# Heads loop of a gated delta rule: recurrence steps, set-up and output norms in another order on all engines

## The reference

```python
L = jnp.where(strict, jnp.einsum('bhncd,bhnsd->bhncs', kb, k) * decay, 0.0)
T = lax.linalg.triangular_solve(eye + L, eye, left_side=True, lower=True, unit_diagonal=True)
u = T @ vb
w = T @ (kb * jnp.exp(g)[..., None])
attn = jnp.einsum('bhncd,bhnsd->bhncs', q, k) * decay
def step(state, inp):
    v_new = u_n - w_n @ state
    o = q_n @ state + a_n @ v_new
    state = state * gl_n + k_n.T @ v_new
o = rmsnorm(o, norm_w) * zg
```

## Time and profile before

| | |
|---|---|
| median of 3 runs | 1715.41 us |
| the profiled execution | 1713.06 us, its span 1711.3 us |
| TensorE busy | 1639.7 us, 96% |
| VectorE, ScalarE, GpSimd busy | 1124.1, 918.6, 489.2 us |
| granted TensorE clock | 0.996 of full in the mean |
| first product of the loop | 220.87 us |
| first output product behind it | 417.41 us |

### The profile page before, as it was taken

One profiled execution on the slowest core, in us unless ns is written; L12 is line 12 of the kernel. 1 busy time (PEld: TensorE's weight loads), 2 busy tenths in 40 slices (PEclk: granted clock), 3 DMA queues, 4 the chain that ended last, 5 costly groups with the idle time before them and its releaser, 6 DMA issues.

```text
span 1711.3 us, 33895 instructions
## 1 busy us (share of the span) xinstructions
PE 1639.7 (96%) x11715; PEld 1523.3 (89%) x11715; DVE 1124.1 (66%) x2320; ACT 918.6 (54%) x1712; POOL 489.2 (29%) x406
## 2 busy tenths in 40 slices
PE   7999999999999989999999999999999999999998
PEld 6899888898988879988999999999999988888886
DVE  4776355554655656367548999978889655555554
ACT  2665523333455555455445444479889744554554
POOL 3000054452700000400006777776666300000000
PEclk9999999999999999999999999999999999999999
DMA  9665411114735324514844555554444456555553
GB/s 295 206 193 174 137 36 50 40 36 144 236 114 148 100 87 149 178 62 137 197 98 137 171 168 167 168 165 134 139 135 140 155 194 195 191 192 194 195 189 131
DMA packets 211817, 255.66 MB, mean 149 GB/s; under 512 B 15912, under 2 KB 193804, under 8 KB 211724
## 3 DMA queue, kind: packets, MB, share of 16 engines
q1 hardware_dynamic: 211723, 254.39, 48.4%
HBM read 253.29 MB, written 1.05 MB: 149 GB/s over the span
## 4 chain that ended last, share of the span: by engine, by line
PE 63%; issue 18%; POOL 10%; DVE 4%; ACT 3%; DMA 1%; SPq 1%; POOLq 0%; DVEq 0%; ACTq 0%
PE ps L2670 20%; PE ps L2108 13%; PE ps L2652 9%; POOL w_lo L716 9%; PE ps L2640 3%; PE ps L2285 3%; PE ps L2284 2%; PE ps L2369 2%; PE ps L2272 2%; PE ps L2128 1%; PE ps L2202 1%; PE ps L2445 1%; DMA arena<-in_ada_w 1%; POOL arena L706 0%; SPq L452 0%
## 5 line engine op out<-in xcount | busy, mean ns | idle before, releaser
L716 POOL TENSOR_TENSOR w_lo<-raw,w_hi 128x1024 fp32r<-128x1024 f32 x128 | 307.8, 2408 | 333.0 <-ACT w_hi L1188 332.8
L2108 PE MATMUL ps<-x_hi,w_hi 128*128 128x256 f32 x1088 | 312.7, 287 | 8.3 <-DVE w_lo L1310 3.0
L2108 PE MATMUL ps<-x_lo,w_hi 128*128 128x256 f32 x1088 | 307.7, 283 | 0.0
L2108 PE MATMUL ps<-x_hi,w_lo 128*128 128x256 f32 x1088 | 307.7, 283 | 0.0
L2067 DVE TENSOR_TENSOR w_lo<-raw,w_hi 128x1024 fp32r<-128x1024 f32 x124 | 152.0, 1226 | 143.3 <-ACT w_hi L1288 143.3
L1288 ACT ACTIVATE w_hi<-raw 128x1024 fp32r<-128x1024 f32 x124 | 131.6, 1061 | 168.0 <-PE ps L2670 168.0
L2108 PEld LDWEIGHTS ps<-x_hi,w_hi 128*128 128x128 f32 x1088 | 208.4, 192 | 14.0 <-issue 4.7
L2108 PEld LDWEIGHTS ps<-x_lo,w_hi 128*128 128x128 f32 x1088 | 208.6, 192 | 0.3 <-issue 0.2
L2108 PEld LDWEIGHTS ps<-x_hi,w_lo 128*128 128x128 f32 x1088 | 208.4, 192 | 0.0
L1188 ACT ACTIVATE w_hi<-raw 128x1024 fp32r<-128x1024 f32 x128 | 134.9, 1054 | 118.1 <-DVE raw L1879 118.1
L2615 PE MATMUL ps<-x_hi,w_hi 128*128 128x256 f32 x576 | 166.2, 288 | 9.9 <-ACT arena L1210 8.9
(11 more groups left out here) (416 smaller groups left out, 3822.4 us busy)
## 6 DMA issues: line engine op xcount, KB each, us to landing
raw<-in_u_experts SPq DMA_DIRECT2D x512, 128.0 KB, 2.6
raw<-in_v_experts SPq DMA_DIRECT2D x128, 512.0 KB, 4.3
arena<-in_ada_w SPq DMA_DIRECT2D x22, 1024.0 KB, 5.3
raw<-in_a_w_in SPq DMA_DIRECT2D x12, 1024.0 KB, 5.4
arena<-in_a_w_in SPq DMA_DIRECT2D x12, 1024.0 KB, 5.4
raw<-in_b_w_in SPq DMA_DIRECT2D x8, 1024.0 KB, 5.7
arena<-in_b_w_in SPq DMA_DIRECT2D x8, 1024.0 KB, 5.5
raw<-in_w_in SPq DMA_DIRECT2D x8, 1024.0 KB, 5.5
```

What stands on the lines that cost most here:

```text
L716: pool.tensor_tensor(UTL[e], UT[e % 2], UTH[e].bitcast(F32), ALU.subtract).then_inc(utl_ready, 1)
L2108: ins = mm(o[:, b * S:b * S + S], w[:, slot, kk, b * P:b * P + P], xx[:, (kk + turn) % KC, :], start=(kk == 0 and n == 0), stop=(kk == k - ...
```

## The change

The same operations are done, in another order. TensorE starts a round with the level-0 products and does the recurrence at levels 0 to 3: step 0 behind the products of level 0, steps 1 and 2 behind the updates of levels 0 and 1, step 3 behind the products of level 2, steps 4 and 5 behind the updates of levels 2 and 3. The keys come at level 1, the rows at level 2, the values at level 3, the modulator between the products and updates of level 4, and x0 between those of level 5. The eight clock-keeping matmuls of round 0 are gone. VectorE follows: keys at level 1, decays and betas at level 2, lower triangles and starts at level 3, the modulator and the first head's norm at level 4; the second head's norm comes in the next round behind the masks of level 0. ScalarE has its two sequences interleaved. The outputs (OS), the norms (RNo) and the exponentials of the decays (EG) have buffers of their own, and the value transposes go to banks 6 and 7. The zeroing of the mask buffer stands ahead of the key norms. The split of the first eight heads goes from round 7's VectorE and ScalarE to GpSimd in round 7 and ScalarE at the end of round 6.

```diff
-        temp(512)
+        EG = [temp(128), temp(128)]
+        OS = [temp(256)]
...
-        SQo = RNo = VN
+        SQo = VN
...
+        OS.append(temp(256))
+        RNo = [temp(256)]
...
+        RNo.append(temp(256))
...
-                    pool.tensor_tensor(QD[r.side][g], QD[r.side][g], r.q[:, 128:256], ALU.mult).then_inc(h_qd, 1)
+                    pool.tensor_tensor(QD[r.side][g], EG[g], r.q[:, 128:256], ALU.mult).then_inc(h_qd, 1)
 
             scores(Round(0))
             for i in range(GQ):
+                if i + 1 == GQ:
+                    for half in range(2):
+                        ks = slice(half * KC // 2, (half + 1) * KC // 2)
+                        pool.wait_ge(xhi_ready, 2 + half + 1)
+                        pool.tensor_tensor(XLO[:, ks, :], ZB[:, ks, :], XHI[:, ks, :].bitcast(F32), ALU.subtract).then_inc(x_split, 1)
...
-            def setup_rows(r):
+            def setup_keys(r):
                 act.wait_ge(g_k0, r.count(1, 1))
                 act.activation(K0, ps[7][:, 0:128], ACT.Copy).then_inc(g_k0s, 1)
                 if r.at:
                     act.wait_ge(h_at, r.count(2))
                 act.activation(KQs, two(ps[7][:, 256:512]), ACT.Copy).then_inc(g_kqs, 1)
+
+            def setup_rows(r):
+                if r.at:
+                    act.wait_ge(h_qd, r.count(2))
                 for g in range(2):
                     act.wait_ge(h_row, r.nth(g))
-                    act.activation(QD[r.side][g], ROWS[g][:, 128:256], ACT.Exp).then_inc(h_eg, 1)
+                    act.activation(EG[g], ROWS[g][:, 128:256], ACT.Exp).then_inc(h_eg, 1)
+
+            def setup_decays(r):
...
-                        act.activation(two(BV[r.side][g])[:, cc, :], A2[g][:, cc * 128:cc * 128 + 128], ACT.Copy,
+                        act.activation(two(BV[r.side][g])[:, cc, :], ROWS[g][:, 256 + cc * 128:384 + cc * 128], ACT.Copy,
...
-            def finish_states(r):
+            def finish_first(r):
...
+            def finish_second(r):
...
             def finish_out(r):
+                if r.at:
+                    act.wait_ge(h_out, r.count(2, 2))
                 for g in range(2):
                     act.wait_ge(h_o, r.nth(g))
-                    act.activation(OS[r.side][g], A2[g], ACT.Copy).then_inc(h_os, 1)
+                    act.activation(OS[g], A2[g], ACT.Copy).then_inc(h_os, 1)
                     act.activation(SQo[g], A2[g], ACT.Square).then_inc(h_sq, 1)
+
+            def finish_norms(r):
...
             def inner(i, f, n):
                 if f:
-                    finish_states(f)
+                    finish_first(f)
+                if n:
+                    setup_keys(n)
+                    setup_rows(n)
+                if f:
+                    finish_second(f)
+                if n:
+                    setup_decays(n)
                 if f:
                     finish_out(f)
                 if n:
-                    setup_rows(n)
                     setup_v(n)
-                    if f:
-                        act.wait_ge(h_out, f.count(2, 4))
+                if f:
+                    finish_norms(f)
+                if n:
                     setup_x0(n)
+                if i.at == GQ - 2:
+                    act.wait_ge(h_out, 2 + GQ)
+                    split_x(1, ZB[:, 0:8, :], 24)
 
             act.wait_ge(g_norm, 4 + 2 * GQ)
+            setup_keys(Round(0))
             setup_rows(Round(0))
+            setup_decays(Round(0))
             setup_v(Round(0))
             setup_x0(Round(0))
             act.wait_ge(raw_free, 8 + N_ADA)
             rounds(inner)
-            act.wait_ge(h_out, 2 + GQ)
-            split_x(1, ZB[:, 0:8, :], 24)
             hi(T_AOUT, 0, 1)
-            finish_states(Round(GQ - 1))
+            finish_first(Round(GQ - 1))
+            finish_second(Round(GQ - 1))
             finish_out(Round(GQ - 1))
+            finish_norms(Round(GQ - 1))
...
+            v.wait_ge(lo_ready, tile_no(T_AOUT, 0, 0))
+            v.memset(zeroed, 0.0)
...
-            def normed(r):
-                for g in range(2):
-                    v.wait_ge(h_orn, r.nth(g))
-                    v.wait_ge(h_os, r.nth(g))
-                    os_ = OS[r.side][g]
-                    v.scalar_tensor_tensor(os_, os_, COLS[:, CAN:CAN + 1], RNo[g], ALU.mult, ALU.mult).then_inc(h_og, 1)
-                for g in range(2):
-                    v.wait_ge(h_og, r.nth(g, 1, 1, 2))
-                    zb = ZB[:, r.heads[g], :]
-                    v.tensor_tensor(zb, OS[r.side][g], zb, ALU.mult).then_inc(h_out, 1)
+            def normed(r, g):
+                v.wait_ge(h_orn, r.nth(g))
+                v.wait_ge(h_os, r.nth(g))
+                v.scalar_tensor_tensor(OS[g], OS[g], COLS[:, CAN:CAN + 1], RNo[g], ALU.mult, ALU.mult).then_inc(h_og, 1)
+                v.wait_ge(h_og, r.nth(g, 1, 1, 2))
+                zb = ZB[:, r.heads[g], :]
+                v.tensor_tensor(zb, OS[g], zb, ALU.mult).then_inc(h_out, 1)
...
             def inner(i, f, n):
                 mask_level(i, 0)
+                if f and f.at:
+                    normed(Round(f.at - 1), 1)
                 close_level(i, 0)
                 mask_level(i, 1)
+                if n:
+                    keys(n)
+                close_level(i, 1)
                 if f:
                     remainder(f)
-                close_level(i, 1)
                 mask_level(i, 2)
+                if n:
+                    decays(n)
                 close_level(i, 2)
+                if n:
+                    betas(n)
                 mask_level(i, 3)
                 if n:
-                    keys(n)
+                    lowers(n)
                 close_level(i, 3)
-                if f:
-                    normed(f)
-                mask_level(i, 4)
-                if n:
-                    decays(n)
-                    betas(n)
-                close_level(i, 4)
-                if n:
-                    lowers(n)
-                else:
-                    split_x(1, ZB[:, 0:8, :])
-                mask_level(i, 5)
                 if n:
                     starts(n)
+                mask_level(i, 4)
+                modulator(i)
+                if f:
+                    normed(f, 0)
+                close_level(i, 4)
+                mask_level(i, 5)
                 close_level(i, 5)
-                modulator(i)
 
             v.sem_inc(h_out, 2)
-            v.memset(zeroed, 0.0)
...
             lo(T_AOUT, 0, 1)
+            normed(Round(GQ - 2), 1)
             remainder(Round(GQ - 1))
-            normed(Round(GQ - 1))
+            for g in range(2):
+                normed(Round(GQ - 1), g)
...
-                    pe.wait_ge(h_eg, r.count(2))
-                    pe.wait_ge(h_xm, r.count(4))
+                    pe.wait_ge(h_bv, r.count(4))
...
-            def setup_values(r, f):
+            def setup_values(r):
+                for g in range(2):
+                    pe.wait_ge(h_eg, r.nth(g))
+                    pe.wait_ge(h_xm, r.nth(g, 1, 0, 2))
+                    for cc in range(2):
+                        ins = pe.transpose(ROWS[g][:, 256 + cc * 128:384 + cc * 128], r.v[g][:, cc * 128:cc * 128 + 128], ident)
+                    ins.then_inc(h_vT, 1)
+
+            def setup_x0(r, f):
                 for g in range(2):
                     if f:
                         pe.wait_ge(h_orn, f.nth(g))
-                    for cc in range(2):
-                        ins = pe.transpose(A2[g][:, cc * 128:cc * 128 + 128], r.v[g][:, cc * 128:cc * 128 + 128], ident)
-                    ins.then_inc(h_vT, 1)
-
-            def setup_x0(r):
-                for g in range(2):
-                    pe.wait_ge(h_bv, r.nth(g, 2))
...
-                    pe.wait_ge(h_xm, n.nth(0, 1, 0, 2))
+                    pe.wait_ge(h_bv, n.nth(0, 2))
...
             def inner(i, f, n):
+                level_p(i, 0)
                 if f:
                     finish(f, 0, i)
-                level_p(i, 0)
+                level_d(i, 0)
                 if f:
                     finish(f, 1)
-                level_d(i, 0)
+                level_p(i, 1)
+                if n:
+                    setup_keys(n)
+                level_d(i, 1)
                 if f:
                     finish(f, 2)
-                level_p(i, 1)
-                level_d(i, 1)
+                if n:
+                    setup_rows(n)
+                level_p(i, 2)
                 if f:
                     finish(f, 3)
-                level_p(i, 2)
+                level_d(i, 2)
                 if f:
                     finish(f, 4)
-                level_d(i, 2)
+                level_p(i, 3)
+                if n:
+                    setup_values(n)
+                level_d(i, 3)
                 if f:
                     finish(f, 5)
-                if f is None:
-                    keep_clock(ps[7][:, 0:P], 8)
-                level_p(i, 3)
+                level_p(i, 4)
```

(17 more changed lines are left out.)

6 lines of the change are left out of this document (2 added, 4 removed).

## The result

The changed kernel takes 1694.76 us in the median of four runs (1694.15 to 1695.60), the kernel before 1715.28 us beside it (1714.07 to 1715.84). The ratio is 0.9881, with a 95% interval of 0.9869 to 0.9893: 20.5 us faster, and 1.8 us above the forecast. The profiled execution took 1694.15 us with a span of 1692.1 us, so the two profiles differ by 19.2 us of span.

A forecast was written before the change was run, and what follows sets the result against it. TensorE was taken to bound nearly everywhere. Start 1.76, round 0 3.53, rounds 1 to 6 13.0, round 7 3.62, output products 0.35 and tile 3 0.37 sum to 22.6 us: from 1715.41 to 1693, range 1688 to 1703.

The forecast's parts named there:

- The steady round: Rounds 1 to 6: 22.45 us each in place of 24.62, 2.17 us less, 13.0 us over six rounds.
- the two named ones: Stalls in a steady round: 0.27 us at level 4's updates, 0.34 us between updates 4 and products 5.
- By a hair: Level 4: first head's norm ends at 19.15 us, closing 4 is due at 19.17, so it costs nothing.
- Round 0: First round, without recurrence or clock-keeping products: 20.44 us against 23.97, 3.53 us less.
- I take full clock: Round 0: the clock is assumed not to fall; if it does, 1.2 us come back.
- The start: Ahead of the loop: moving the 1.76 us mask-buffer fill into VectorE idle time brings the first product 1.76 us earlier.
- Round 7: Last round to the first output product: 21.2 us against 24.82, 3.62 us less.
- does meet GpSimd and may take 1.6 us in place of 0.85: Second head's late norm, behind mask 0: ends at 3.0 us, closing 0 at 3.4, before products 1 at 3.57; hidden.
- Nothing, by half a us: GpSimd's split in round 7 costs nothing: sums end at 15.4 to 15.5 us, modulator due at 16.0.
- Rival 2: Clock falls in round 0 or at the end, or round 7 waits for GpSimd's split: 1695 us; chance 0.16.
- GpSimd's end: Steady round: GpSimd works until 13.3 us or so, 3 us before the starts on VectorE.
- Output products and tile 3: After the loop: 0.35 us from output products at full clock, 0.37 us from tile 3's shorter wait for weights.

The follow-up runs named there:

- experiment 7: Changed kernel with TensorE's x0 transposes put back behind the updates of level 5: 1699.62 us, ratio to before 0.9919.
- experiment 8: Changed kernel with recurrence step 0 put back in front of the level-0 products: 1699.32 us, ratio to before 0.9923.
- experiment 6: Changed kernel with both heads' norms behind the modulator at level 4, none behind mask 0: 1692.38 us, ratio to before 0.9878.
- experiment 4: Changed kernel with the zero fill of the mask buffer put back behind the key norms: 1696.37 us, ratio to before 0.9891.
- experiment 1: Changed kernel with GpSimd's split of round 7 behind its last sums in place of in front: 1691.52 us, ratio to before 0.9861.
- experiment 2: Changed kernel with GpSimd's split in the same place, cut into eight operations in place of two: 1689.57 us, ratio to before 0.9859.
- experiment 5: Changed kernel with GpSimd's split of round 7 as one operation in place of two: 1694.74 us, one run (before 1713.23).
- experiment 9: Changed kernel with GpSimd's split behind its sums and x0 between updates 4 and products 5: 1691.04 us, ratio to before 0.9860.
- experiment 10: Changed kernel with round 0's eight clock-keeping matmuls back in front of the products of level 3: 1694.78 us, ratio to before 0.9886.
- experiment 12: Changed kernel with GpSimd's split behind its last sums, measured again beside the changed kernel (1694.57 us): 1693.12 us, ratio to before 0.9870.
- the last set: The third set of runs, experiments 9 to 12, which includes the changed kernel itself (1694.57 us); the kernel before took 1714.59 us.
- experiment 3: Changed kernel with the zero fill of the mask buffer directly in front of the key norms: 1694.69 us, ratio to before 0.9887.

## Why the prediction was right, and where not

- **The steady round** was right by its steps: 22.375 us for 22.45. The stalls left are the two named ones (level 4's was 0.21 us for 0.27). That the others went for the named reasons is shown by putting two of them back: x0 (experiment 7) 0.72 us, step 0 (experiment 8) 0.62 us a round. "By a hair" for the first head's norm is shown by experiment 6.
- **Round 0**: 20.41 for 20.44. "I take full clock" held, with the clock-keeping products or without.
- **The start**: 1.59 us for 1.76, and 1.97 in experiment 4. The waits shrank as said, but the clock fell even so, in front of x0 instead of behind it. It fell in five of the thirteen profiles behind the change (both of the changed kernel, experiments 1, 2 and 4) and held in eight. It cost 0.46 us: from the fill's start to the first product it is 31.25 us in the changed kernel, and 30.79 in experiments 5 to 10 and 12, whose clock held.
- **Round 7 is the step that failed**: "Sum 21.2 against 24.82: 3.62 us less" was -0.97, so 4.6 us of the forecast gain didn't come. The 21.2 itself is right, as experiment 1 shows (21.35). What failed is the sentence on the late norm, that it "does meet GpSimd and may take 1.6 us in place of 0.85", and that on the split, "Nothing, by half a us". I sized the meeting by a factor of two from the starts of round 0, whose neighbours on GpSimd are short operations (0.6 to 1.0 us), and looked at the split only for when it ends, though the prediction has both at the same place: the norm from 1.38, the split until 5.7. In round 7 the neighbour is the split itself, 2.4 us an instruction, and the norm took 4.56 us: 2.8 us on the path and 1.6 more by the clock.
- **Rival 2** gave 1695 for a wait in round 7 and a fall of the clock there. Both came, through VectorE and not through TensorE's wait for the split. The changed kernel took 1694.76, so the number itself fits this rival as well as the forecast.
- **GpSimd's end** was off by 2.2 us, since I overlooked that the scores wait for the outputs of step 4. It cost nothing: starts and scores stay 0.75 us apart.
- **Output products and tile 3**: 0.7 for 0.72.
- The forecast stood on one profile of before. Its clock was a good one: the runs of before at a mean clock of 0.993 took 1716.0 to 1716.2 us in the last set, the two at 0.996 took 1712.9 and 1714.3. So the profiles differ by less than the medians, 19.2 against 20.5 us.
- **Luck**: the parts that the change touches gave 18.4 of 22.6 us. What brings this to the 20.5 us of the medians is none of the prediction's: 2.1 us behind tile 3, 1.5 of them the clock of the second layer, and 1.3 by which the medians differ more than the profiles, less 1.3 for the offset of the front. That the time is only 1.8 us from 1693 is partly luck. Without these it would be about 1697, still inside 1689 to 1698.

## What to carry to other kernels

When an operation of VectorE with two SBUF inputs moves, look up what GpSimd runs beside it, and count the length of one GpSimd instruction for each of VectorE's, not the shares of busy time; if both must overlap, cut GpSimd's work in short instructions. Count the last round of a loop by its own neighbours, since what stands there only once is missing from the steady round. And where two versions differ by a few us, compare stretches of the trace at the same granted clock before the medians.

## What the runs showed of the hardware

An operation of VectorE whose two inputs are in SBUF ends just behind the GpSimd instruction under way at its start: 0.61 and 0.72 us beside multiplies of about 0.6 to 0.8, 0.83 beside a piece of 0.91, 2.11 and 2.45 beside 2.36 and 2.52, 4.75 beside 4.50. Taken one by one, 294 of 308 such operations between 240 and 400 us of the fourteen profiles end 0.28 us behind that instruction, however long it is. Ten more began so near its end that their own 0.47 us lasted longer, and four waited out the next multiply too. GpSimd pays as well: its next instruction lasts 0.79 us in place of 0.61 for a multiply and 0.91 in place of 0.73 for a piece. With one input in PSUM VectorE isn't held: closings took 0.41 us beside the same multiplies and pieces. The Trainium skill's SBUF — State Buffer (Who interferes with whom) says that VectorE and GpSimd share one pair of ports, and that the second of two such instructions fully blocks until the first ends. The traces agree, by the durations just given. The prediction had weighed only the milder sentence of the Trainium skill's GPSIMD Engine Reference (section 1, Specifications), which names contention and no price; by the stricter one the norm would have ended with the split, which the prediction had at 5.7 us of the round, and closing 0 at 6.1, where the products of level 1 want it at 3.57: the wait of 2.5 us.

The clock fell behind a wait of 2.54 us in round 7 in three profiles (both of the changed kernel and experiment 3's) and held behind the same wait in experiments 4 and 10. It fell behind one of only 1.93 us in experiment 8, and held behind one of 2.92 us in experiment 7. At the 2.74 us wait in layer 2 it fell in experiment 1 and held in the changed kernel. So the length of the wait alone doesn't decide it, and what does, these profiles don't show. A fall cost 0.5 us at the start, 1.6 in round 7, and 2.0 in the second layer of experiments 4, 5 and 6. The remaining short stalls of a steady round (0.1 to 0.34 us) never moved it from 1.00.
